# Attention denominators of blocks 12 to 15: from a spread by the matrix engine to rows read back from DRAM

## The reference, cut to what matters

```python
def _sink_attend(q, k, v, mask, sink):
    s = einsum('bqhgd,bkhd->bhgqk', q, k) * HEAD_DIM ** -0.5     # masked to the window
    m = maximum(max(s, axis=-1), sk)
    p = exp(s - m[..., None])
    den = sum(p, axis=-1) + exp(sk - m)
    o = einsum('bhgqk,bkhd->bqhgd', p, v)
    return o / den
# then: x + gate * ((o * silu(g)) @ w_out)
```

## Time and profile before

| | us |
|---|---|
| median of 3 runs | 2662.75 |
| lowest, highest | 2661.27, 10594.77 |
| the profiled execution | 2663.45 |
| its span, first to last instruction | 2661.6 |
| PE busy in the span | 2588.9 (97%) |
| DVE, ACT, POOL busy | 1187.3, 894.4, 646.4 |

### The profile page before, as it was taken

How to read it: one execution, slowest core, us unless ns; L and a number is a source line. 1 busy time by engine, 2 the same in 40 slices (tenths; PEclk the granted TensorE clock), 3 DMA queues, 4 the chain that set the end, 5 groups by cost and what they waited for, 6 DMA issues and landing times. The chain is left out here.

```text
span 2661.6 us, 49945 instructions
## 1 busy us (share of the span) xinstructions
PE 2588.9 (97%) x18699; PEld 2268.2 (85%) x18699; DVE 1187.3 (45%) x3262; ACT 894.4 (34%) x2110; POOL 646.4 (24%) x833
## 2 busy tenths in 40 slices
PE   6899999999999999999999999999999999999998
PEld 3688888888889887787999999999999999998786
DVE  3646646465464656552233342514233342515433
ACT  3445626345362654222222131312222131313211
POOL 2522131232213212332022130403122030403332
PEclk8999999999999999999999999999999999999999
DMA  9512031120212214442022220313122120416443
GB/s 358 212 51 78 17 90 30 53 79 29 74 36 71 61 56 151 135 135 74 23 50 80 38 83 18 85 44 74 47 48 82 38 83 17 86 43 163 159 144 110
DMA packets 187838, 219.66 MB, mean 83 GB/s; under 512 B 27248, under 2 KB 132480, under 8 KB 185680
## 3 DMA queue, kind: packets, MB, share of 16 engines
q1 hardware_dynamic: 177616, 189.11, 25.4%
q10 hardware_dynamic: 9984, 27.37, 2.7%
HBM read 178.27 MB, written 38.17 MB: 81 GB/s over the span
## 5 line engine op out<-in xcount | busy, mean ns | idle before, releaser
L521 PE MATMUL psum<-h_hi,m_w_lo 128*128 128x384 f32 (+1 forms) x1600 | 594.0, 371 | 1.1 <-ACT gt_nat L1408 1.1
L523 PE MATMUL psum<-h_hi,m_w_hi 128*128 128x384 f32 (+1 forms) x1600 | 573.7, 359 | 0.0
L522 PE MATMUL psum<-h_lo,m_w_hi 128*128 128x384 f32 (+1 forms) x1600 | 573.1, 358 | 0.0
L523 PEld LDWEIGHTS psum<-h_hi,m_w_hi 128*128 128x128 f32 x1600 | 300.5, 188 | 27.0
L521 PEld LDWEIGHTS psum<-h_hi,m_w_lo 128*128 128x128 f32 x1600 | 301.3, 188 | 26.0 <-issue 1.6
L522 PEld LDWEIGHTS psum<-h_lo,m_w_hi 128*128 128x128 f32 x1600 | 301.6, 189 | 22.5
L521 PE MATMUL psum<-h_hi,attn_w_lo 128*128 128x384 f32 (+1 forms) x800 | 291.9, 365 | 0.9 <-DVE attn_w_lo L506 0.6
L523 PE MATMUL psum<-h_hi,attn_w_hi 128*128 128x384 f32 (+1 forms) x800 | 285.7, 357 | 0.0
L522 PE MATMUL psum<-h_lo,attn_w_hi 128*128 128x384 f32 (+1 forms) x800 | 285.5, 357 | 0.0
L894 ACT ACTIVATE arena<-arena,stats 128x640 f32<-128x640 f32 (+2 forms) x272 | 213.4, 786 | 74.0 <-DVE stats L976 73.0
L976 DVE CUSTOM_DVE_ANT_0 arena<-psum,wmask,stats 128x640 f32<-128x640 f32 (+2 forms) x256 | 206.1, 839 | 58.7 <-PE psum L1172 58.2
(11 more groups left out here) (317 smaller groups left out, 4669.1 us busy)
## 6 DMA issues: line engine op xcount, KB each, us to landing
m_bc<-gate_rows_mlstm SPq DMA_DIRECT2D x128, 256.0 KB, 3.4
m_w_raw<-in_mlstm_w_in SPq DMA_DIRECT2D x40, 512.0 KB, 4.7
h_full<-gated_output SPq DMA_DIRECT2D x29, 512.0 KB, 4.1
gated_output<-gT SPq DMA_DIRECT2D x8, 1088.0 KB, 5.2
layer_output<-xb_out ACTq DMA_DIRECT2D x17, 512.0 KB, 2.7
h_hi_full<-layer_output SPq DMA_DIRECT2D x17, 512.0 KB, 4.8
out<-h_hi_full ACTq DMA_DIRECT2D x17, 512.0 KB, 4.9
xb<-in_x_sample ACTq DMA_DIRECT2D x16, 512.0 KB, 6.7
```

Of the source, the lines that this page charges most:

```text
L521: pe.matmul(out, self.lo[:, k, :], E.h_hi[:, k, tok], start=(k == 0), stop=False)
L522: pe.matmul(out, self.hi[:, k, :], E.h_lo[:, k, tok], start=False, stop=False)
L523: ins = pe.matmul(out, self.hi[:, k, :], E.h_hi[:, k, tok], start=False, stop=(k == KT - 1))
```

## The change

Blocks 12 to 15 become a fourth quad in the half-stages 0 to 6; only block 16 is still spread there. The last half-stage (`LAST`) keeps three quads and five lone blocks. The fourth quad's `scale` stands at the end of the half-stage in POOL's list, behind block 16's `rspr` copy. In SP's list its write and its two reads stand behind the first two rotary loads of the next stage, ahead of `store`. The semaphore counts follow.

```diff
-        QUADS = 3
-        LONE = 4 * QUADS
+        QUADS = 4
+        LAST = 2 * NKV - 1
+        quads_of = lambda i: 3 if i == LAST else QUADS
+        lone_of = lambda i: 4 * quads_of(i)
+        lone_before = lambda i: i * (NT - 4 * QUADS)
+        ALL_QUADS = LAST * QUADS + quads_of(LAST)
...
                 def store(kv, sub):
-                    sp.wait_ge(s_scaled, at((kv * 2 + sub + 1) * QUADS))
+                    i = kv * 2 + sub
+                    sp.wait_ge(s_scaled, at(i * QUADS + quads_of(i)))
...
-                    recip_rows(kv, 0)
+                    recip_rows(kv, 0, range(3))
                     rotary(kv, 3, 0)
                     rotary(kv, 3, 1)
+                    recip_rows(kv, 0, range(3, QUADS))
                     store(kv, 0)
...
-                        recip_rows(kv, 1)
+                        recip_rows(kv, 1, range(3))
                         rotary(kv + 1, 0, 0)
                         rotary(kv + 1, 0, 1)
+                        recip_rows(kv, 1, range(3, QUADS))
                     store(kv, 1)
...
-                                if b >= LONE:
+                                if b >= lone_of(kv * 2 + sub):
...
+                            if quads_of(kv * 2 + sub) == QUADS:
+                                scale(QUADS - 1)
...
-                            if b < LONE and b % 4 == 3:
+                            if b < lone_of(kv * 2 + sub) and b % 4 == 3:
...
-                        if b >= LONE:
-                            pe.wait_ge(s_rs, at((kv * 2 + sub) * (NT - LONE) + b - LONE + 1))
+                        if b >= lone_of(kv * 2 + sub):
+                            pe.wait_ge(s_rs, at(lone_before(kv * 2 + sub) + b - lone_of(kv * 2 + sub) + 1))
...
-    E.recip_dram = dram("reciprocals_by_token", [2 * NKV, 3, 2, 4 * P])
+    E.recip_dram = dram("reciprocals_by_token", [2 * NKV, 4, 2, 4 * P])
```

More of the change, by code:

```diff
@@ L687, in rotary, with recip_rows @@
                     sp.dma_start(cs[b][0:rows, :, 0:wl], E.a["rotary"][0:rows, :, t0:t0 + wl]).then_inc(s_cs[b], 16)
-                def recip_rows(kv, sub):
+                def recip_rows(kv, sub, quads):
                     i = kv * 2 + sub
                     sp.wait_ge(s_rope, at(kv * ROPES + NG * (2 + sub)))
-                    for r in range(QUADS):
+                    for r in quads:
                         n = i * QUADS + r
@@ L751, in _ @@
                         sp.wait_ge(s_pT, at(NKV * (2 * NU)))
-                        sp.wait_ge(s_scaled, at(2 * NKV * QUADS))
+                        sp.wait_ge(s_scaled, at(ALL_QUADS))
                         sp.dma_start(spare[:, 5:KT, :], w_out[:, 5:KT, :]).then_inc(s_wo, 16)
@@ L807, in head @@
                                     pool.wait_ge(s_ogl, at(16 * (n + 1)))
-                                    pool.wait_ge(s_scaled, at((2 * NKV - 1) * QUADS + 1))
+                                    pool.wait_ge(s_scaled, at(LAST * QUADS + 1))
                                     settle(E, pool)
@@ L996, in denominators @@
                                 dve.wait_ge(s_rq, at((kv * 2 + sub) * QUADS))
-                                dve.wait_ge(s_rs, at((kv * 2 + sub) * (NT - LONE)))
+                                dve.wait_ge(s_rs, at(lone_before(kv * 2 + sub)))
                             if b == CTX:
@@ L1008, in gate @@
                                 dve.tensor_copy(rturned[:, :], E.bank[6][0:8, P:2 * P]).then_inc(s_rt, 1)
-                            if b < LONE:
+                            if b < lone_of(kv * 2 + sub):
                                 dve.scalar_tensor_tensor(g, weighted, 0.5, g, ALU.mult, ALU.mult).then_inc(s_og, 1)
@@ L1012, in gate @@
                             dve.scalar_tensor_tensor(g, spread, 0.5, g, ALU.mult, ALU.mult).then_inc(s_gr, 1)
-                            dve.wait_ge(s_gr, at((kv * 2 + sub) * (NT - LONE) + b - LONE + 1))
+                            dve.wait_ge(s_gr, at(lone_before(kv * 2 + sub) + b - lone_of(kv * 2 + sub) + 1))
                             dve.tensor_tensor(g, weighted, g, ALU.mult).then_inc(s_og, 1)
```

## The result

The changed kernel takes 2674.2 us in the median of 8 runs, against 2663.3 for the kernel before: a ratio of 1.0037, interval 1.0028 to 1.0046, or +10.9 us. It is slower by less than half a percent, 7 us above the predicted 2667.0 and just inside the range.

What follows compares the result with a forecast made beforehand. The prediction took PE, busy 97% of the span, to bound the kernel. Saving 5.0 us on PE, adding 8.9 in kv stages and 0.4 in q stages, gave +4.3 on 2662.75: 2667.0 us, range 2660 to 2675.

Steps and rivals of the forecast that it cites:

- saved on PE: Seven changed half-stages: four transposes less, one more, net 0.72 us each, 5.0 us less in all.
- kv stages: Three stages: late store delays the weights' low half; PE waits 2.6 us more, plus 0.35 each, 8.9 us in all.
- q stages: Four stages behind sub 0: late first shuffle nearly made good, 0.1 us each, 0.4 us in all.
- rival 2: Clock falls during the three new kv-stage waits, 3.4 us lost each, 10.2 more, 2677.2 us; chance 0.11.
- the lower bound of 0.5: PE saving per half-stage if ACT's copies hold PE where it would now be early; 3.5 us in all.
- The way out and back: Fourth quad's write, reads and product after gate(15), about 6.4 us, making the store 3.65 us late.
- The slow writes: Fourth quad's DRAM write in sub 1 slower by 0.7 us in half the cases; 0.35 us per kv stage.
- Whether DVE gets in between two instructions of POOL: At the weights' low half in kv stages: it does, so PE waits 2.6 us more; otherwise 3.7.
- Rival 1: Hidden slack in the kv-stage chain covers the late store; only PE's saving remains, 2657.7 us; chance 0.12.
- Rival 3: Over 2% slower (53 us), PE also waiting for the first bank once the round trip grows 3.5 us; chance 0.02.
- Rival 4: DVE doesn't get between POOL's instructions in kv stages: 1.1 us more each, 2670.3 us; no separate chance.
- the likeliest case: Whole kernel: PE saving plus kv and q stage waits, 2667.0 us, bounds 2661 to 2676; chance 0.75.

Runs made afterwards that it cites:

- no_way_back: Changed kernel without the fourth quad's write, read back and product, blocks 12 to 15 of half-stages 0 to 6 left undivided; 0.9983 of the kernel before.
- late_store_3: Kernel before, with three small DRAM writes in SP's list ahead of the store of sub 1 (kv 0 to 2); 1.0048 of the kernel before.
- late_store_6: Kernel before, with six small DRAM writes in SP's list ahead of the store of sub 1 (kv 0 to 2); 1.0092 of the kernel before.
- changed_again: The changed kernel run once more, nothing altered, beside the others on one chip; 1.0033 of the kernel before.
- sub1_only: Changed kernel with the fourth quad only in the three half-stages of sub 1 that precede a kv stage; 1.0041 of the kernel before.

## Why the prediction was right or wrong

The direction and the mechanism were right, and so was the largest term. The size came out at 10.9 instead of 4.3 because three smaller terms were off, all the same way.

| term | predicted | attention stretch of the profile |
|---|---|---|
| saved on PE | -5.0 | -3.0 (no_way_back) |
| kv stages | +8.9 | +8.6 (9.2 less 0.6) |
| q stages | +0.4 | +2.8 |
| clock | 0, rival 2 | +3.4 (2 falls of 1.7) |
| sum | +4.3 | +11.8, measured +11.6 |

**What is taken off PE.** Mis-sized, at 0.72 per half-stage where 0.43 is right, just under the lower bound of 0.5. The bound named a cause, ACT's copies holding PE, but I took the middle; it is shown for block 13, where it takes 0.15 us. The rows for it were in the trace: ACT's copy ended at 457.03 and `turn(15)` began at 457.49, 0.46 later, and the two transposes ahead of it that fell away took 0.52. That copy stands in ACT's list behind block 15's exponentials, which hang on scores ahead of both removed transposes, so it could not move with PE. That a wait is 0 before says nothing of how far PE can run ahead of it.

**The way out and back.** Right: 6.60 us from `gate(15)` to the store against 6.4, the store 3.84 late against 3.65. The slow writes, 0.35 per kv stage in the sum, did not occur: in all seven fourth quads the read followed the write by 1.21 or 1.22 us, while 5 of the changed kernel's 24 other quads had 1.5 to 2.3. That half the writes of sub 1 are slow does not carry over to a quad at another place, and I cannot say why they are slow. The fit of the Trainium skill, page DMA: Bandwidth & Descriptors, section Anatomy of one DMA, by which the prediction gave an estimate beside its sum (2.0 us for the write), is for DMAs issued by GpSimd. These are issued by SyncE, and the write took 1.2 us.

**The kv stages.** Right in mechanism and size: waits of 2.89, 2.86 and 3.45, of which 0.2 was there before, against 2.6 and 0.35 for slow writes. Their release of the first bank held nobody, as forecast. Whether DVE gets in between two instructions of POOL was the choice between 2.6 and 3.7, and it did:

```profile
364.21 0.99 POOL L830 TENSOR_TENSOR arena<-arena 64x384 f32<-64x384 f32 x1 [1.33 <-DVE kT L957]
...
364.69 1.07 DVE L506 TENSOR_TENSOR attn_w_lo<-attn_w_raw,attn_w_hi 128x512 fp32r<-128x512 f32 x1
...
365.28 1.33 POOL L835 TENSOR_TENSOR kT<-kT,arena 64x384 f32<-64x384 f32 x1
```

DVE ended 0.55 us after POOL's first product and PE started at 365.90. POOL's second would have kept it until 366.3 or later, even at the 1.00 us that this instruction took a unit earlier instead of 1.33. late_store_3 confirms the place, since a late store alone makes the same waits. That the sum fits so closely, 8.6 for 8.9, is luck in part: the slow writes, 1.05 in it, did not come, and a store that landed 0.56 late did.

**The q stages.** The step that failed is the chain's time to the weights' low half. I had it end at 485.64 against 485.63, with no room for error, and took 0.1. In the trace:

```profile
472.83 0.28 DVE L1017 COPY rturned<-psum 8x128 f32<-8x128 f32 x1 [2.70 <-PE psum L1218]
...
479.57 0.74 DVE L954 STREAM_SHUFFLE arena<-psum 128x512 f32<-128x512 f32 x1
...
491.56 0.60 DVE L954 STREAM_SHUFFLE arena<-psum 128x384 f32<-128x384 f32 x1
...
492.74 0.69 DVE L506 TENSOR_TENSOR attn_w_lo<-attn_w_raw,attn_w_hi 128x512 fp32r<-128x512 f32 x1
```

The first shuffle comes 6.74 us behind `gate(15)`, predicted 6.4, since POOL's product begins 0.1 us later and its hand-over to DVE takes 0.3 us, where I had counted 0.05. From it to unit 3's shuffle the chain takes 11.99, predicted 11.96, and from there to the end of the low half 1.87, predicted 1.74. The low half ends at 493.43, 20.60 behind `gate(15)`; before, it was 20.07. With no slack, each tenth is PE's, and so are the 0.7 us by which one read landed late (the wait of 1.22). The cover that I had counted on was just used up.

**The rivals.** Rival 1, the wait hidden, fell: no profile of the changed kernel has it. Rival 3 did not come. Its point, a way out and back of 9.9 us, was not reached by the changed kernel; late_store_6 has its store 10.0 us behind `gate(15)`, and PE still shows no wait for the first bank. Nothing later was run. Rival 4 did not come. Rival 2, the clock, came true in part. I had held against it that the new waits are shorter than the 4.1 us one; waits of 2.8 us are long enough more often than not. Its price was half of what I had said, 1.7 us a fall in most cases instead of 3.4: the row I took it from stands behind a longer wait and had 6.8 us at the lower level, most of these have 3.4 (one in changed_again cost 3.1). I treated it as another world with a chance of 0.11, when it was a term to be added to the likeliest case with its odds. That cost 3 to 6 us, and it also widens the runs: 2671 to 2678 us.

**The shape of the forecast.** "Same" at 0.97 was right, and the range of 2660 to 2675 held 2674.2 with 0.8 to spare. That was luck in part. Its upper end was made of slow writes, of DVE not getting in and of 3.2 us in the q stages; the first two did not come, and the falls of the clock, which the range was meant to leave out, filled their place.

## What to carry to other kernels

When a step is moved out of a loop to its end, look for what its last result lets go: here the store, and through DVE's ordered list the weights of a stage that shares no data with it. The store's first twelve blocks of 17 did not need the late result; cutting a transfer where its data become ready, and giving the late rows a buffer of their own, turned a loss of 10.9 us into a gain of 5.6 to 5.9. Where a chain ends within 0.1 us of being late, price it as late, and add to every new wait of PE the chance that the clock falls behind it.

## What the runs showed of the hardware

The granted clock can fall behind waits of PE much shorter than expected: behind 9 of 14 waits between 2.7 and 3.7 us, all three of 6.0 to 6.3, one of 4.5 and one of 1.86. At the same length it falls or not: 2.86 us had both. The Trainium skill, page TensorE: Matmul & The Clock Gate, part on the clock gate, has the clock halved after idling; the trace agrees, with 0.50 in the window from 368 to 370 us of the changed kernel's profile. Behind waits under 5 us a fall cost 1.7 us in most cases and up to 3.1 (0.69 over 10 us) in one. In late_store_6 the clock was already low during the wait (0.50 from 364.20 to 367.30 us).

A 4 KB write to DRAM was followed by the dependent read 1.2 to 1.3 us after its issue in most cases of the two kernels, and 1.4 to 2.3 us in others. The 1088 KB store behind the half-stages 0 to 6 landed 5.2 to 5.4 us after its issue, but for 5.8 once in the changed kernel, 6.0 once in no_way_back and 6.8 once in sub1_only; in the first and the last of these a kv stage followed, and PE's wait there was 0.6 and 1.7 us longer than in the others. What makes these slow was not tried and is left open.

A DVE `tensor_tensor` with two SBUF inputs that began under a POOL `tensor_tensor` was done 0.55 us after it, between two POOL instructions that follow each other at 0.08 us (365.20 and 365.28 us of the changed kernel's profile); in the earlier trace rows it was done 0.27 us after it.
